# A two-layer decoder trunk: tiles of 256 bytes or more are placed at multiples of 256 bytes, small tiles in front

## The reference

```python
for l in range(DEPTH):                       # 2
    mod = silu(c) @ w_mod[l] + b_mod[l]      # 6 x 1024 modulation columns
    h = rmsnorm(x) * (1 + sc1) + sh1
    z = h @ w_in[l]                          # 36 panels of 128 columns
    # three causal mixers (spatial gating, latent attention, windowed pooling)
    merged = sum_i sigmoid(gate_i) * (mixer_i @ w_i)
    x = x + g1 * (merged @ w_o[l])
    h2 = rmsnorm(x) * (1 + sc2) + sh2
    # PEER: 8 heads pick 16 of 16384 experts per token
    q = h2 @ w_pq[l]; scores -> top-16 -> expert indices, softmax weights g
    a = gelu(<u_tab[expert], h2>)
    x = x + g2 * sum_k g_k * a_k * v_tab[expert_k]
return rmsnorm(x) * final_norm
```

## Time and profile before

| | |
|---|---|
| median of 3 runs | 3517.16 us (3514.73 to 3519.53) |
| profiled execution, span from first to last instruction | 3511.6 us |
| TensorE matmul busy | 3448.3 us (98%), 17974 records |
| VectorE busy | 2418.7 us (69%) |
| ScalarE busy | 1400.6 us (40%) |
| GpSimd busy | 1372.5 us (39%) |
| moved by DMA | 910.04 MB, 259 GB/s over the span |

### The profile page before, as it was taken

The page is one execution under the profiler, slowest core; times in us unless marked ns, Lnnn a source line. Parts: engine busy times, 40 slices in busy tenths (PEclk is TensorE's granted clock), DMA queues, the critical chain, the costliest instruction groups (busy, mean ns, idle before and its releaser), DMA issues.

```text
span 3511.6 us, 53302 instructions
## 1 busy us (share of the span) xinstructions
PE 3448.3 (98%) x17974; PEld 2925.7 (83%) x17974; DVE 2418.7 (69%) x4725; ACT 1400.6 (40%) x2298; POOL 1372.5 (39%) x1291
## 2 busy tenths in 40 slices
PE   7999999999999999999999999999999999999999
PEld 5776799999999877777777777999999998777777
DVE  6455679999887865555464566899998868555554
ACT  3334244343576332332333333434346753332232
POOL 1011108667743434444400110277668325344442
PEclk9999999999999999999999999999999999999999
DMA  6375447776899989999735743577779999899995
GB/s 239 118 257 183 144 135 228 215 226 189 263 344 324 387 304 350 353 354 348 297 128 178 229 149 130 189 220 207 208 226 278 345 337 368 313 359 350 357 350 185
DMA packets 306403, 910.04 MB, mean 259 GB/s; under 512 B 69076, under 2 KB 101892, under 8 KB 305316
## 3 DMA queue, kind: packets, MB, share of 16 engines
q0 software_dynamic: 163792, 473.58, 39.8%
q1 hardware_dynamic: 105552, 383.83, 31.6%
q10 hardware_dynamic: 36868, 50.35, 3.9%
HBM read 792.14 MB, written 115.47 MB: 258 GB/s over the span
## 4 chain that ended last, share of the span: by engine, by line
PE 90%; DVE 3%; DMA 2%; POOL 2%; issue 2%; ACT 1%; ACTq 0%; SPq 0%; DVEq 0%; POOLq 0%
PE ps L461 15%; PE ps L463 14%; PE ps L462 14%; PE ps L1078 10%; PE ps L1080 10%; PE ps L1079 10%; PE ps L1092 3%; PE ps L1058 3%; PE ps L881 2%; PE ps L978 1%; PE ps L937 1%; PE ps L979 1%; PE ps L980 1%; PE ps L1018 1%; POOL weight_spill L757 1%
## 5 line engine op out<-in xcount | busy, mean ns | idle before, releaser
L461 PE MATMUL ps<-mov,whl 128*128 128x384 f32 (+1 forms) x2816 | 1007.1, 358 | 1.1 <-DVE whl L448 1.1
L463 PE MATMUL ps<-mov,whl 128*128 128x384 f32 (+1 forms) x2816 | 986.7, 350 | 0.0
L462 PE MATMUL ps<-mov,whl 128*128 128x384 f32 (+1 forms) x2816 | 986.1, 350 | 0.0
L448 DVE TENSOR_TENSOR whl<-raw,whl 128x1024 fp32r<-128x1024 f32 x648 | 793.5, 1225 | 220.1 <-ACT whl L438 215.6
L438 ACT CAST whl<-raw 128x1024 fp32r<-128x1024 f32 x648 | 679.7, 1049 | 102.6 <-ACT hst L1273 96.4
L1078 PE MATMUL ps<-whl,wgthl 128*128 128x512 f32 x1536 | 611.3, 398 | 3.4 <-DVE wgthl L1817 3.3
L1080 PE MATMUL ps<-whl,wgthl 128*128 128x512 f32 x1536 | 609.1, 397 | 0.0
L1079 PE MATMUL ps<-whl,wgthl 128*128 128x512 f32 x1536 | 603.8, 393 | 0.0
L461 PEld LDWEIGHTS ps<-mov,whl 128*128 128x128 f32 x2816 | 529.7, 188 | 39.1 <-issue 8.7
L463 PEld LDWEIGHTS ps<-mov,whl 128*128 128x128 f32 x2816 | 529.0, 188 | 31.5
L462 PEld LDWEIGHTS ps<-mov,whl 128*128 128x128 f32 x2816 | 529.9, 188 | 30.2 <-issue 2.2
(11 more groups left out here) (271 smaller groups left out, 3645.5 us busy)
## 6 DMA issues: line engine op xcount, KB each, us to landing
raw<-in_uT_tab SPq DMA_DIRECT2D x256, 512.0 KB, 4.1
raw<-in_v_tab SPq DMA_DIRECT2D x256, 512.0 KB, 6.9
expert_spill<-hst ACTq DMA_DIRECT2D x256, 192.0 KB
hin<-expert_spill POOLq DMA_DIRECT2D x256, 192.0 KB, 7.3
gt<-weight_spill POOLq DMA_DIRECT2D x64, 768.0 KB, 8.6
raw<-in_w_in SPq DMA_DIRECT2D x72, 512.0 KB, 5.4
raw<-in_w_mod SPq DMA_DIRECT2D x64, 512.0 KB, 3.6
weight_spill<-stage POOLq DMA_DIRECT2D x14, 2048.0 KB, 13.3
```

The source lines that it names most:

```text
L448: nc.vector.tensor_tensor(whl[:, m % RING, 1], raw[:, raw_n(m) % RAW], whl[:, m % RING, 0].bitcast(F32), ALU.subtract).then_inc(lo_done, 1)
L461: nc.tensor.matmul(o, w[:, 0, k], src[:, 0, k, :cols], start=(k == 0), stop=False)
L462: nc.tensor.matmul(o, w[:, 0, k], src[:, 1, k, :cols], start=False, stop=False)
L463: mm = nc.tensor.matmul(o, w[:, 1, k], src[:, 0, k, :cols], start=False, stop=(k == KC - 1))
```

## The change

`sb()` rounds the start of a tile of 256 bytes or more up to a multiple of 256, and demands the same of a start given with `at=`. The small tiles (columns of parameters, of sums and maxima) are asked for first, the large ones after them, and the top of the memory is rounded up wherever a start is kept to be used again.

```diff
+LINE = 256
...
         size += -size % 32
-        off = top_of[0] if at is None else at
         if at is None:
+            if size >= LINE:
+                top_of[0] += -top_of[0] % LINE
+            at = top_of[0]
             top_of[0] += size
-        return nc.alloc_sbuf_tensor_at(name, shape, dt, offset=off)
...
+        elif size >= LINE:
+            assert at % LINE == 0, (name, at)
+        return nc.alloc_sbuf_tensor_at(name, shape, dt, offset=at)
...
     mod = sb("mod_cols", [P, N_MOD])
     bmod = sb("bmod", [P, N_MOD])
-    c_act = sb("c_act", [P, D])
     fin = sb("fin", [P, KC])
-    ident = sb("ident", [P, P])
-    identr = sb("identr", [P, P], F32R)
...
     rinv = sb("rinv", [P, 2])
+
+
+    x_sb = sb("x_sb", [P, KC, S])
+    top_of[0] += -top_of[0] % LINE
+    mov_at = top_of[0]
+    mov = sb("mov", [P, 2, KC, S], F32R)
+    vrow = sb("vrow", [P, VR, D], at=mov_at)
+    raw = sb("raw", [P, RAW, KC, P])
+    whl = sb("whl", [P, RING, 2, KC, P], F32R)
...
+    top_of[0] += -top_of[0] % LINE
     free = top_of[0]
...
+    top_of[0] += -top_of[0] % LINE
     y_at = top_of[0]
```

More of the change, by code:

```diff
@@ L253, in build_trunk @@
     rinv4 = sb("rinv4", [P, TT])
-    cos = sb("cos", [P, TT, HALF])
-    sin = sb("sin", [P, TT, HALF])
     gain = sb("gain", [P, 5])
@@ L265, in build_trunk @@
     rinv = sb("rinv", [P, 2])
+    x_sb = sb("x_sb", [P, KC, S])
[5 more added lines that the diff above has]
+    whl = sb("whl", [P, RING, 2, KC, P], F32R)
+    c_act = sb("c_act", [P, D])
+    ident = sb("ident", [P, P])
+    identr = sb("identr", [P, P], F32R)
+    ones = sb("ones", [P, P])
+    top_of[0] += -top_of[0] % LINE
+    causal_at = top_of[0]
+    causal = sb("causal", [P, P])
+    zero = sb("zero", [P, P], at=causal_at)
+    ident16 = sb("ident16", [P, P], BF16)
+    causal16 = sb("causal16", [P, P], BF16)
+    iota = sb("iota", [P, P])
+    cos = sb("cos", [P, TT, HALF])
+    sin = sb("sin", [P, TT, HALF])
+    top_of[0] += -top_of[0] % LINE
     sq_at = top_of[0]
```

## The result

The changed kernel takes 3479.53 us (3477.28 to 3481.46, 4 runs) against 3515.94 us before (3513.65 to 3519.53, 4 runs): ratio 0.9902, interval 0.9889 to 0.9914, or 36.4 us less. The forecast was 3484 us. The profiled spans are 3477.0 and 3511.6 us. The numbers of instructions and of DMA packets are the same.

A forecast was written before the change was run, and what follows sets the result against it. TensorE bounds the kernel (busy 98%), so time is matmuls times step plus some 60 us. Terms -33.3 + 0.5 - 0.5 gave -33.3 us, so 3517.2 - 33.3 = 3484 us, range 3476 to 3518.

The forecast's parts named there:

- (a): Matmuls with mrg and wgthl: 4992 fall from 233.3 to 226.7 ns, 33.3 us less, 30.7 of it in the value stage.
- the first reason: Float32r matmuls with one operand 32 off a multiple of 64 and the other not pay 6.67 ns more.
- The sum: All terms added: -33.3 + 0.5 - 0.5 = -33.3 us, the +0.5 being loss in the value stage while rows are gathered.
- (b): The 9024 matmuls of mov with whl, moved from 128 past to 0 past: no change, costed at 0.
- The floor: Rival: the fixed 13.3 ns per float32r matmul also goes, in part or wholly; 3407 us (3340 to 3450), chance 0.07.
- 0 past a worse start than 128: Rival: mov with whl loses 60 us and (a) gives nothing; 3577 us, chance 0.04.
- the one that put the pace on the half of the memory: Rival: operands above or below byte 131072, or the kind of tile, set the 6.67 ns; 3516 us, chance 0.20.
- (c): Plain float32 matmuls, as L881 at 430 ns for 512 columns: nothing to win, 0, at most 1 us.
- (d): VectorE: operands at different starts take 1219 to 1225 ns, so starts do nothing there, 0.
- (e): DMA transfers: SyncE's loads are early and hidden by a ring of four; only the head gains, -0.5 us.

The follow-up runs named there:

- wgthl_only: The kernel before with one edit, wgthl begun at a multiple of 256 (the buffers behind it move along); 3512.97 us, ratio 0.9997.
- same_remainder_128: The kernel before with mrg and wgthl begun 128 past a multiple of 256, as whl and mov already were; 3482.13 us against 3513.89, ratio 0.991.
- all_32_again: The changed kernel with every large tile 32 bytes past a multiple of 256, run on one chip with three others; 3484.59 us, ratio 0.9914 to before.
- probe_pairs: The changed kernel with 36 runs of 24 filler matmuls behind its end, at various offsets, widths and types; only their paces are read, not the time.
- all_128_past: The changed kernel with every large tile 128 bytes past a multiple of 256; 3486.54 us, ratio 0.9913 to before.
- after_again: The changed kernel itself, unaltered, run again as the yardstick of one chip; 3477.75 us, ratio 0.9894 to before.

## Why the prediction was right, and where it was not

The time came within 5 us of the forecast, and the steps fell as it said. The reason for the fall was wrong, and what was missed nearly cancels: losses in the value stages and behind `mrg`, and a gain by the transfers.

**(a) `mrg` and `wgthl`: size right, reason wrong.** 233.3 fell to 226.7 ns in both, as forecast. "One operand 32 off a multiple of 64 and the other not" was the step that failed. It fitted the four pairs at hand, but so did "different remainders modulo 256", and the trace before had no pair to part them. wgthl_only did: by the first reason 30.7 us, measured none. The right reading is the difference modulo 256, shown from both sides: same_remainder_128 gets the gain without moving any tile to a multiple of 256, wgthl_only misses it with one. The change works since it makes all remainders equal; that this satisfies the wrong reason too is luck. By the wrong reason the smaller edit of wgthl_only would have brought nearly as much as the change.

**The 27.9 us of 30.7 in the value stages.** TensorE's idle time there rose from 3.8 to 5.5 us (the stretches above, length less busy). The DMA share stayed at 0.90 and moved 347 GB/s in place of 339, so the transfers nearly kept up. The sum had 0.5 us of loss there; it was 2.8.

**What `mrg` gave was lost behind it.** Its 192 matmuls in a layer take 44.3 us in place of 45.3, as forecast. But from the last of them to the first matmul of the head stage, where TensorE waits for sums, it took 10.5 us in place of 9.3, in both layers. The rows are this stretch in the kernel before, in the changed one, in wgthl_only and in layer 2 of all_32_again:

```profile
442.77:452.03 9.26, 7.25 (x37) 6.00 (x35) 4.64 (x8) 2.45 (x5) 0.53 (x1) 0.82 0.45 162
```

```profile
441.00:451.51 10.51, 8.50 (x37) 7.29 (x35) 4.62 (x8) 2.42 (x5) 0.53 (x1) 0.68 0.43 143
```

```profile
444.21:454.74 10.53, 8.52 (x36) 7.31 (x35) 4.57 (x8) 2.38 (x5) 0.54 (x1) 0.68 0.39 142
```

```profile
2156.81:2165.97 9.16, 7.15 (x37) 6.08 (x36) 4.05 (x7) 2.28 (x4) 0.53 (x1) 0.81 0.46 166
```

The work is the same; the granted clock (third from the right) is 0.82 or 0.68, a mean of the levels 1.2 and 2.4 GHz, and the small matmuls take longer at the lower one: eight records of L505 took 1.03 us before, and on its line in the changed kernel, L524, 1.83. This is no price of the faster `mrg`. wgthl_only, with `mrg` still slow, has the long stretch, and all_32_again, with `mrg` fast, has the long one in layer 1 and the short one in layer 2. So a trace shows either of the two, 1.3 us apart, and the 1.1 us of `mrg` are real where the clock is equal. The forecast had no term for it.

**(b) `mov` with `whl` at 0: right.** 226.5 and 173.3 ns after. The floor did not fall, nor was 0 past a worse start than 128; with these two rivals goes the one that put the pace on the half of the memory, since `wgthl` is above byte 131072 and `whl` below in both kernels. The 215.8 ns that the prediction set beside them are bfloat16's pace, which probe_pairs shows at each of its four offsets; float32r has its own.

**(c), (d): right.** L881's eight records take 3.44 us after as before; VectorE's panel takes 1225 ns, `urow` 1219.

**(e) the DMAs: the term that was mis-sized.** I took 0.5 us in the head, and SyncE's loads behaved so: the first matmul with `mrg` starts 0.7 us sooner (396.74 in place of 397.43). But I had looked only at SyncE's loads and at the waits that name one. GpSimd's packets, which the term left out, became 2% cheaper: 39.2% of 3477.0 us in place of 39.8% of 3511.6. The comparison on one chip puts the whole at 7 to 9 us by the medians and at about 5 at equal clock.

Where in the kernel that time is won is not settled. The stretches from L1058 to the value stage, with a DMA share of 0.96, lost 3.6 and 2.1 us. In layer 1 the waits of TensorE that went are one for `hotg` (2.2 us to 0.4) and one for `wgthl` (1.1 to none); in layer 2, 1.0 of the 2.1 us is a wait of L1058 that no transfer ends ("issue", 3.0 to 2.0). And all_128_past, with the dear packets, takes 225.0 and 224.2 us from its first L1058 to the value stage, the changed kernel 224.1 and 224.7. What grows in the traces of all_32_again and all_128_past is TensorE's wait for `wgthl`: 6.7 and 5.3 us in all, against 3.4 in after_again. Its factors come through GpSimd's queue, and there `hin` lands in 8.0 and 7.5 us in place of 7.0 at the median. Of the tiles only `stage` was tried alone.

The Trainium skill ("DMA: Bandwidth & Descriptors", How a descriptor splits into AXI transactions) has the direction for GpSimd's queue: the first transaction of a descriptor that is off a 256-byte boundary starts at the boundary below it, and the bytes before its start are paid for. It would have 128 past cost more than 32, as more bytes lie before the start; the two queues took 1386 and 1387 us, alike. For SyncE's 4096-byte rows at 128 past the same rule gives 3%, an estimate from it, and no run shows that (1100 us, and 1108 at 0); there the measurement decides.

## What to carry to other kernels

Where float32r matmuls of 512 columns fill TensorE, take the pace from starts of unbroken runs and compare it between pairs of tiles; place the moving and the stationary tile at the same remainder modulo 256, which here was worth 6.7 ns a matmul, 33 us of steps in all. Do not take equal remainders for a law at other widths: measure the width in use. Where the DMA engines are full, put the tiles that GpSimd's queue reads or writes at multiples of 256; here that was worth some 5 us of 3480. Before two medians of such kernels that differ by less than 10 us are compared, look at the granted clock of their runs. When a rule is read off a few pairs, list every rule that fits them, and try one placement in which they differ before the rule is named.

## What the runs showed of the hardware that I had not expected

- With starts at multiples of 32 bytes, the step of a 512-column float32r matmul depends on the difference of the two starts modulo 256 (226.7 ns at 0, 229 to 234 otherwise), while bfloat16 (215.8 ns) and plain float32 (429.2 ns) had one pace at the four offsets tried.
- At 448 columns the equal remainder is the slow one: 206.7 ns against 200.0 at a difference of 160. At 384 it makes 0 to 3 ns.
- The same bytes in the same packets of GpSimd's queue cost 2% less DMA time with tiles at multiples of 256; SyncE's queue shows no such gain.
- One and the same stretch of waits and small matmuls takes 9.2 us at a granted clock of 0.82 and 10.5 at 0.68, and a kernel can show both in one execution (all_32_again).
